# Two blocks of a sequence model on one core: the first modulation goes to TensorE in column groups, and the conv stage's taps and output columns are reordered

## The reference

```
mod   = silu(c) @ w_ada + b_ada            # 6 vectors of 1024; the context has its own, from c_ctx
h     = rmsnorm(x, g_mix) * (1 + scale1) + shift1     (and hc from ctx with the context's vectors)
z     = h @ w_in     # q, k, v, g, dd (decay rank), and three conv and two gate parts
gated linear attention in two directions, started from the context's states; 3-wide conv branch
x     = x + gate1 * (sigmoid(ga)*y_gla + sigmoid(gb)*y_conv) @ w_mix_out
x     = x + gate2 * swiglu(modulate(rmsnorm(x)));  x = rmsnorm(x)
second block: conv/pool mixer (31-wide causal depthwise conv on 512 channels, layernorm, silu,
              window means on the other 512, @ w_out), swiglu, HGRN2 mixer, swiglu, rmsnorm
```

## Time and profile before

| what | us |
|---|---|
| median of 3 runs | 2304.03 (2303.44 to 2307.84) |
| the profiled execution | 2308.86 |
| its span, first to last instruction | 2307.1 |
| PE busy | 2188.2 (95%) |
| DVE / ACT / POOL busy | 1024.4 / 885.7 / 910.2 |

### The profile page before, as it was taken

How to read it: one execution, slowest core, us unless ns; L and a number is a source line. 1 busy time by engine, 2 the same in 40 slices (tenths; PEclk the granted TensorE clock), 3 DMA queues, 4 the chain that set the end, 5 groups by cost and what they waited for, 6 DMA issues and landing times.

```text
span 2307.1 us, 29442 instructions
## 1 busy us (share of the span) xinstructions
PE 2188.2 (95%) x10644; PEld 1763.1 (76%) x10644; DVE 1024.4 (44%) x1421; ACT 885.7 (38%) x1310; POOL 910.2 (39%) x445
## 2 busy tenths in 40 slices
PE   3899999989998999999999999999899989999997
PEld 1788677668886888888757888888688877888886
DVE  7403566565445222212876333300577756333201
ACT  5313435453324222233355233322566645332222
POOL 5222232224444444344543444444322315444442
PEclk8899999999998999999999999999999989999999
DMA  6312121215552322233312322233212213322231
GB/s 240 110 64 64 46 73 41 69 55 189 202 205 87 109 91 100 77 95 92 114 37 74 104 96 94 79 99 111 65 64 73 73 37 104 97 94 97 79 100 67
DMA packets 64703, 217.36 MB, mean 94 GB/s; under 512 B 7008, under 2 KB 8160, under 8 KB 64384
## 3 DMA queue, kind: packets, MB, share of 16 engines
q1 hardware_dynamic: 64640, 216.52, 28.7%
HBM read 214.40 MB, written 2.10 MB: 94 GB/s over the span
## 4 chain that ended last, share of the span: by engine, by line
PE 69%; DVE 5%; ACT 3%; issue 2%; DMA 1%; DVEq 0%; ACTq 0%; SPq 0%
PE ps L473 22%; PE ps L474 21%; PE ps L475 21%; DVE acc L1633 1%; PE ps L767 1%; PE ps L857 1%; DVE h_lo L1596 1%; DMA x_res<-in_x 1%; ACT w_hi L947 0%; ACT h_hi L1146 0%; DVE hs L1878 0%; PE ps L709 0%; PE ps L624 0%; DVE x L1608 0%; PE ps L636 0%
## 5 line engine op out<-in xcount | busy, mean ns | idle before, releaser
L361 POOL TENSOR_TENSOR w_lo<-w_raw,w_hi 128x1024 fp32r<-128x1024 f32 (+2 forms) x376 | 856.7, 2287 | 1341.5 <-ACT w_hi L947 1341.2
L473 PE MATMUL ps<-h_hi,w_lo 128*128 128x512 f32 x1920 | 757.3, 394 | 16.1 <-DVE h_lo L1654 5.0
L475 PE MATMUL ps<-h_hi,w_hi 128*128 128x512 f32 x1920 | 750.8, 391 | 0.0
L474 PE MATMUL ps<-h_lo,w_hi 128*128 128x512 f32 x1920 | 750.6, 391 | 0.0
L947 ACT ACTIVATE w_hi<-w_raw 128x1024 fp32r<-128x1024 f32 (+2 forms) x376 | 370.9, 995 | 507.3 <-PE ps L475 504.4
L473 PEld LDWEIGHTS ps<-h_hi,w_lo 128*128 128x128 f32 x1920 | 363.0, 189 | 100.7 <-DVE h_lo L1654 6.6
L475 PEld LDWEIGHTS ps<-h_hi,w_hi 128*128 128x128 f32 x1920 | 362.3, 189 | 76.5
L474 PEld LDWEIGHTS ps<-h_lo,w_hi 128*128 128x128 f32 x1920 | 363.1, 189 | 74.5 <-issue 0.7
L473 PE MATMUL ps<-gu_hi,w_lo 128*128 128x512 f32 x528 | 205.4, 389 | 0.0
L474 PE MATMUL ps<-gu_lo,w_hi 128*128 128x512 f32 x528 | 205.4, 389 | 0.0
L475 PE MATMUL ps<-gu_hi,w_hi 128*128 128x512 f32 x528 | 205.4, 389 | 0.0
(11 more groups left out here) (330 smaller groups left out, 2469.2 us busy)
## 6 DMA issues: line engine op xcount, KB each, us to landing
w_raw<-in_w_ffn_in SPq DMA_DIRECT2D x132, 512.0 KB, 3.4
ada_w<-in_w_ada SPq DMA_DIRECT2D x48, 512.0 KB, 4.9
w_raw<-in_w_hg SPq DMA_DIRECT2D x40, 512.0 KB, 3.4
w_raw<-in_w_ffn_out SPq DMA_DIRECT2D x48, 384.0 KB, 3.1
w_raw<-in_w_conv_gate SPq DMA_DIRECT2D x32, 512.0 KB, 3.4
w_raw<-in_w_merge SPq DMA_DIRECT2D x32, 512.0 KB, 5.1
w_raw<-in_w_ffn_out SPq DMA_DIRECT2D x48, 320.0 KB, 2.9
w_raw<-in_w_cp SPq DMA_DIRECT2D x20, 512.0 KB, 3.4
```

Source lines behind the costliest of these rows:

```text
L361: pool.tensor_tensor(w_lo[s][:, 0:n], raw[s][:, 0:n], w_hi[s][:, 0:n].bitcast(F32), ALU.subtract).then_inc(lo_done[s], 1)
L473: pe.matmul(out, wl, hi, start=first, stop=False)
L474: pe.matmul(out, wh, lo, start=False, stop=False)
L475: return pe.matmul(out, wh, hi, start=False, stop=last)
```

## The change

**First stage.** The first 2048 columns of `w_ada` are laid out on the host as eight tiles of 128 x (8 x 256): for slice k, the shift and the scale columns. `mod_sums(k)` on PE multiplies them with `cond_pad` (silu of both conditions, padded with zeros to 32 columns): eight f32 matmuls, the chunk j of the inputs writing to the 32 output partitions from 32 j, two chunks accumulated in each. DVE copies the four partial rows out of PSUM (`turn_in`), two small matmuls with a selection matrix `pick` add them and turn them into columns (`mod_turn`), DVE adds the bias and makes `amp1`. DVE (not POOL) now multiplies with `rstd0` and the amplitude in one operation (`value`), ACT adds the shift and rounds (`h1_hi`), DVE takes the low half with the shift in one operation (`low`); only then does it copy the sums for slice k + 2. The squares of x are added in pairs on DVE, so that PE has four matmuls of ones and not eight.

SP loads x first in four pieces, then weight unit and modulation tile in turn, ctx last, and `w_up` only behind `dd_hi`. PE works by pairs (unit, slice): stage k takes slice k for the units so far and all slices so far for unit k (the decay product is unit 4). The context is normalized behind that: its squares are summed inside the last stage, its slices are split by ACT between the reads of q and by DVE; units 4 and 5 run latents, latents, context, context, and then the decay product of the context. The two first units of the next round are converted in `act_start`. The forget gate's small vectors (`lb`, `om_lb`) are made at the end of the qkv stage.

**Conv stage.** The first four tap matrices are made by ACT ahead of its last four weight conversions; the sums of groups 0 and 1 are issued after 24 taps, group 3 ahead of group 2. In the output, slices 0 and 1 go over all units as before, then PE waits for all low halves and finishes unit after unit with slices 2 and 3.

Elsewhere semaphores are only shared or renumbered. The diff, without removed lines (they stand in the code above), cut to its core:

```diff
+    sp.dma_start(cond_col[:, :, :], dram["cond_cols"]).then_inc(S["small_in"], 16)
+    for i in range(4):
+        sp.dma_start(x_all[:, 2 * i:2 * i + 2, 0:T], dram["x"][:, 2 * i:2 * i + 2, :]).then_inc(S[f"x_in{i}"], 16)
     sp.dma_start(vec[:, :], dram["vectors"]).then_inc(S["vec_in"], 16)
+    def ada(k):
+        if k >= 4:
+            sp.wait_ge(S["ada1_used"], k - 3)
+        sp.dma_start(ada1_w[k % 4][:, :, :], dram["w_ada_first"][k]).then_inc(S[f"ada_full{k % 4}"], 16)
+    for s in range(4):
+        sp_unit(sp, s, 0, dram["w_qkv"][0, s])
+        ada(s)
     sp.dma_start(dd_raw[:, :], dram["w_decay"]).then_inc(S["dd_in"], 16)
+    for k in range(4, KC):
+        ada(k)
+    sp.dma_start(x_all[:, :, T:TC], dram["ctx"]).then_inc(S["x_in0"], 16)
     sp.wait_ge(S["const_step"], 1)
+    sp.wait_ge(S["dd_hi"], 1)
     for d in range(2):
         sp.dma_start(w_up[16 * d:16 * d + 16, d, :, :], dram["w_dec_up"][d]).then_inc(S["dd_in"], 16)
...
+    step(pool.memset(cond_pad[:, :, :], 0.0))
...
+    for j in range(3):
+        step(pool.tensor_tensor(pick[:, :], (pick if j else ident)[:, 0:2], ident[:, 32 * j + 32:32 * j + 34], ALU.add))
...
+def pool_first(pool):
+    for s in range(4):
+        pool_lo(pool, s, 0)
     pool.wait_ge(S["dd_hi"], 1)
     pool.tensor_tensor(dd_lo[:, :], dd_raw[:, :], dd_hi[:, :].bitcast(F32), ALU.subtract).then_inc(S["dd_split"], 1)
...
+    def mod_sums(k):
+        pe.wait_ge(S[f"ada_full{k % 4}"], 16 * (k // 4 + 1))
+        if k == 0:
+            pe.wait_ge(S["cond_ready"], 1)
+        if k == 1:
+            pe.wait_ge(S["norm_rstd"], 1)
+        if k >= 2:
+            pe.wait_ge(S["mod_row"], k - 1)
+        for t in range(2):
+            for j in range(4):
+                rows = slice(32 * j, 32 * j + 32)
+                mm = pe.matmul(ps[rows, 5 - k % 2, 0:2 * P], cond_pad[:, j + 4 * t, :], ada1_w[k % 4][:, j + 4 * t, :],
+                               start=(t == 0), stop=(t == 1), skip_group_check=True)
+        mm.then_inc(S["ada1_used"], 1)
+    def mod_turn(k):
+        pe.wait_ge(S["mod_row"], k + 1)
+        if k:
+            pe.wait_ge(S["mod1_ready"], 2 * k - 1)
+        for n in range(2):
+            mm = pe.matmul(ps[:, 7, 4 * k + 2 * n:4 * k + 2 * n + 2], mod_row[k % 2][:, n * P:(n + 1) * P], pick[:, :],
+                           start=True, stop=True, skip_group_check=True)
+        mm.then_inc(S["mod_turned"], 1)
+    begun = set()
+    def pair(s, k):
         pe.wait_ge(S["h_lo"], k + 1)
+        if s < 4:
+            if s not in begun:
+                pe.wait_ge(lo_done[s], 1)
+            mm = products(pe, ps[:, s, :], s, k, h1_hi[:, k, :], h1_lo[:, k, :], s not in begun, k == KC - 1)
+            if k == KC - 1:
+                mm.then_inc(unit_done[s], 1)
+        else:
+            if s not in begun:
+                pe.wait_ge(S["dd_split"], 1)
+            decays(ps[:, 6, :], k, h1_hi, h1_lo, s not in begun)
+        begun.add(s)
...
+    def stage(k):
+        if k > 4:
+            return [(s, k) for s in range(5)]
+        return [(s, k) for s in range(k)] + [(k, i) for i in range(k + 1)]
+    def pairs(some):
+        for s, k in some:
+            pair(s, k)
+    for i in range(4):
+        pe.wait_ge(S["norm_pair"], i + 1)
+        pe.matmul(ps[:, 4, :], ones[:, :], sq0[2 * i][:, :], start=(i == 0), stop=(i == 3)).then_inc(S["sq0_mm"], 1)
+        if i == 2:
+            mod_sums(0)
+    for k in (0, 1):
+        mod_turn(k)
+        mod_sums(k + 1)
+    for k in range(KC - 2):
+        work = stage(k)
+        if k:
+            mod_sums(k + 2)
+        if k == 0:
+            mod_turn(2)
+            pairs(work)
+        else:
+            pairs(work[:1])
+            mod_turn(k + 2)
+            pairs(work[1:])
+    pairs(stage(6))
+    pairs(stage(7)[:1])
+    pe.wait_ge(S["mod_row"], KC - 1)
+    for k in range(KC):
+        pe.wait_ge(S["ctx_sq"], k + 1)
+        pe.matmul(ps[:, 5, 0:CTX], ones[:, :], sqc[k % 6][:, :], start=(k == 0), stop=(k == KC - 1))\
+          .then_inc(S["sq0_mm"], 1)
+    pairs(stage(7)[1:])
...
+    def lat(u):
         s, q, bank = u % 4, u // 4, u % 2
         pe.wait_ge(lo_done[s], q + 1)
         pe.wait_ge(S["qkv_lat_read"], u if u >= 6 else u - 2)
         for k in range(KC):
+            products(pe, ps[:, bank, :], s, k, h1_hi[:, k, :], h1_lo[:, k, :], k == 0, k == KC - 1)
+    def context(u):
+        s, bank = u % 4, u % 2
+        pe.wait_ge(*((S["qkv_ctx_read"], u - 5 if u < 8 else u - 4) if u >= 6 else (S["qkv_lat_read"], u)))
         for k in range(KC):
+            if u == 4:
+                pe.wait_ge(S["split_lo"], k + 1)
        ...
...
+    lat(4)
+    lat(5)
+    context(4)
+    context(5)
+    pe_decay_ctx(pe)
+    for u in range(6, 16):
+        lat(u)
+        context(u)
...
+    def ln_sum(j, sem, n, first=False, last=False):
+        pe.wait_ge(S[sem], n)
+        return pe.matmul(ps[:, 5, :], ones[:, :], cv[:, j, :], start=first, stop=last)
     pe.wait_ge(S["conv_in0"], 2)
     for i in range(CONVW):
+        if i == 24:
+            ln_sum(0, "conv_end", 1, first=True)
+            ln_sum(1, "conv_end", 2)
         pe.wait_ge(S["tap_ready"], i + 1)
         pe.matmul(ps[:, 4, :], tap[i % 4][:, :], a_sb[:, 2, i:i + T], start=(i == 0), stop=(i == CONVW - 1))\
           .then_inc(S["tap_mm"], 1)
+    ln_sum(3, "conv_end", 3)
+    ln_sum(2, "conv_pe", 1, last=True).then_inc(S["ln_sum"], 1)
...
+    for k in range(2):
+        pe.wait_ge(S["cat_lo"], CPC + k + 1)
         for s in range(4):
+            output(s, k)
+    pe.wait_ge(S["cat_lo"], CPC + CPC)
+    for s in range(4):
+        output(s, 2)
+        output(s, 3).then_inc(unit_done[s], 1)
...
 def act_start(act):
     act.wait_ge(S["small_in"], 16)
     act.wait_ge(S["const_ready"], 1)
+    act.activation(cond_pad[:, :, 0:2], cond_col[:, :, :], ACT.Silu).then_inc(S["cond_ready"], 1)
     for k in range(KC):
+        if k % 2 == 0:
+            act.wait_ge(S[f"x_in{k // 2}"], 16)
+        act.activation(sq0[k][:, :], x_all[:, k, 0:T], ACT.Square, scale=ROOT).then_inc(S["norm_sq"], 1)
+    act_hi(act, 0, 0)
+    act.activation(spare[:, 8:9], ones[:, 0:1], ACT.Ln)
+    act.wait_ge(S["sq0_mm"], 4)
+    act_rstd(act, 0, rstd0[:, 0:T], ps[:, 4, :])
+    def ctx_squares(first, last):
+        for k in range(first, last):
+            if k >= 6:
+                act.wait_ge(S["sq0_mm"], 4 + k - 5)
+            act.activation(sqc[k % 6][:, :], x_all[:, k, T:TC], ACT.Square, scale=ROOT).then_inc(S["ctx_sq"], 1)
+    for k in range(KC):
         act.wait_ge(S["h_val"], k + 1)
+        act.activation(h1_hi[:, k, :], nv0[k % 2][:, :], ACT.Identity, bias=mod1[:, k, 0:1]).then_inc(S["h_hi"], 1)
+        if k < 3:
+            act_hi(act, k + 1, 0)
+        if k == 3:
+            act.wait_ge(S["dd_in"], 16)
+            act.activation(dd_hi[:, :], dd_raw[:, :], ACT.Copy).then_inc(S["dd_hi"], 1)
+    act.wait_ge(S["x_in0"], 32)
+    ctx_squares(0, 6)
+    act_hi(act, 0, 1)
+    ctx_squares(6, KC)
+    act.activation(spare[:, 8:9], ones[:, 0:1], ACT.Ln)
+    act.wait_ge(S["sq0_mm"], 4 + KC)
+    act_power(act, rstd0[:, T:TC], ps[:, 5, 0:CTX], S["ctx_rstd"], 0)
+    act_hi(act, 1, 1)
+def act_ctx(act, first, last):
+    for k in range(first, last):
+        act.wait_ge(S["split_val"], k + 1)
+        act.activation(hc_hi[:, k, :], nvc[k % 2][:, :], ACT.Identity, bias=mod1[:, k, 1:2]).then_inc(S["split_hi"], 1)
...
+        if u == 2:
+            act.wait_ge(S["dd_mm"], 1)
+            act.activation(dd_sb[:, 0:T], ps[0:32, 6, :], ACT.Copy).then_inc(S["qkv_lat_read"], 1)
...
+            act_ctx(act, 2 * u, 2 * u + 2)
...
 def act_cp(act):
+    def tap_weights(i):
+        act.activation(tap[i % 4][:, :], ident[:, :], ACT.Copy, scale=v_at("dw_w", 2 * CONVW + i))\
+           .then_inc(S["tap_ready"], 1)
     for r in range(2):
         q = 2 * r + Q_CPI
         for p in range(2):
             act.wait_ge(S["cp_scaled"], 4 * r + 2 * p + 1)
             act.activation(csg[p][:, :], csg[p][:, :], ACT.Sigmoid).then_inc(S[f"conv_sg{p}"], 1)
+            if r == 1 and p == 0:
+                for i in range(4):
+                    tap_weights(i)
             act_hi(act, 2 * p, q + 1)
             act_hi(act, 2 * p + 1, q + 1)
         if r == 0:
             for s in range(4):
                 act_hi(act, s, Q_CPI + 2)
+    for i in range(4, CONVW):
+        act.wait_ge(S["tap_mm"], i - 3)
+        tap_weights(i)
...
+    for i in range(4):
+        dve.wait_ge(S["norm_sq"], 2 * i + 2)
+        dve.tensor_tensor(sq0[2 * i][:, :], sq0[2 * i][:, :], sq0[2 * i + 1][:, :], ALU.add).then_inc(S["norm_pair"], 1)
+    def turn_in(k):
+        dve.wait_ge(S["ada1_used"], k + 1)
+        dve.tensor_copy(mod_row[k % 2][:, :], ps[:, 5 - k % 2, 0:2 * P]).then_inc(S["mod_row"], 1)
+    def modulation(k):
+        both = slice(k, 2 * KC, KC)
+        dve.wait_ge(S["mod_turned"], k + 1)
```

(54 more changed lines are left out.)

228 lines of the change are left out of this document (69 added, 159 removed).

## The result

| | before | after |
|---|---|---|
| median, us | 2305.94 (2303.44 to 2314.06, 4 runs) | 2276.2 (2274.87 to 2278.52, 4 runs) |
| the profiled execution, its span | 2308.86, 2307.1 | 2274.92, 2273.2 |
| mean granted clock | 0.979 | 0.986 |

The ratio is 0.9866 [0.9839, 0.9894]: 29.7 us faster by the medians. Two later comparisons of the same pair gave 0.987 [0.9848, 0.9892] and 0.9865 [0.985, 0.988], 31.9 and 30.6 us. The forecast was 2276.7, a gain of 27.3.

The account below looks back on a forecast made before the run. PE, busy 95% of 2307.1 us, bounds the kernel, so only its waits matter. First stage 20.1 plus conv stage 7.2 gives 27.3 us gained, from a median of 2304.03 to 2276.7; range 2266 to 2293.

Parts of the forecast that it names:

- The round: First stage, PE: eight f32 mod_sums matmuls in four column groups take 1.9 us; ends 3.43 and 0.86.
- rival (A): Modulation rounds: four column groups run at once, 0.86 instead of 1.9 us a round; 2271 or 2268 us; chance 0.20.
- The clock: First stage: PE without gaps from 35 to 70 us at a granted clock of 1.00.
- Rival (C): First stage: PE sinks to the 1.2 GHz level and stays, +28 us, 2304 to 2305; chance 0.05 shared with (E).
- The start: First stage: slice 0 high at 23.9 us, its low half at 24.7; first product at 24 to 26.
- The slices: First stage: the first four slices come 5.2 us apart, as amp must wait for POOL's weight split.
- Stretched in slices 0 to 3: First stage, sign to look for on DVE: amp stretched in slices 0 to 3 and short behind.
- What is late next: Ahead of unit 4: PE waits 2.5 us for q_sb, plus 1.3 us for 1.2 GHz behind it.
- Nothing lost behind it: Behind the first stage: later w_qkv loads cost nothing; moved lb/om_lb chain nothing, or 2 us without cover.
- (B): First stage: column groups don't overlap, or DVE loses POOL turns at values and low halves; 2284 to 2293 us; chance 0.25.
- (D): First stage: low clock and column groups one behind another, 6.9 us a round; slower, 2324 us; chance 0.05.
- (E): Order of queues: added matmuls and taps aren't where the diff puts them; no size; chance 0.05 shared with (C).

Follow-up runs that it names:

- e4: The changed kernel, unchanged, profiled again as the measure for other runs on the same chip; 2276.11 us.
- e7: The changed kernel plus extra 128-column PE matmuls on constants into an unread bank, filling PE's waits in the first stage; 2273.11 us, one run.
- e5: The changed kernel with all eight matmuls of a modulation round in column group 0, three quarters of the inner sum left out; 2291.9 us, one run.
- e3: The changed kernel with ACT reading q of units 0 and 1 around the context's root, ahead of a weight split; 2272.76 us against 2276.11.
- e10: The kernel before with only the conv output's new column order, without the early taps and sums; 2306.03 us, one run, against 2306.63.
- e1: The changed kernel with the conv stage of before, so only the first stage changed; 2281.09 us against 2308.01 for the kernel before, ratio 0.9889.

## Why the prediction was right

**First stage, 20.1 forecast, 21.3 measured.** The path was the one described, but two terms were off and made up for each other. From the low half of slice 0 (24.7 forecast) to the end of the stage (70.4) the prediction has 45.7 us. The profiled execution has 22.92 to 68.64, again 45.7, but by shorter rounds and a lower clock; e4 and e7 have 43.6. That the stage came so close is in part luck.

- *The round.* 1.9 us were forecast, from the 1.8 times of two groups. It takes 1.07, so four groups run 3.4 times as fast as one (e5). This was rival (A)'s mechanism, at a little less than its size; the estimate of 1.1 from the Trainium skill (TensorE: Matmul & The Clock Gate, Part 3: Packing small matmuls) was the better one, and its rule on program order cost nothing. Six rounds at 0.83 less are 5.0 us. With the clock at 1.00 (e7) the stage ended at 66.3, 4.1 ahead of the 70.4 forecast. Two rounds of the profiled execution did take 1.94, near the forecast 1.9, but because of the low clock.
- *The clock.* 1.00 was forecast from 35 us on, and so it was from 40; but it was 0.53 and 0.78 from 20 to 40, which no term held. The profiled execution ended the stage 68.64 - 66.31 = 2.3 us later than e7, 2.1 of it behind slice 0. e4's 1.6 us stand ahead of slice 0, in the sums of squares, where the prediction did reckon with the low clock. Rival (C) had the mechanism but priced it at 28 us: PE had enough to do for the clock to come back by itself. The reading behind it left out one window, where the kernel before had shown that too:

```profile
50.00:60.00 10.00, 4.16 (x16) 3.13 (x14) 9.82 (x9) 4.49 (x8) 10.00 (x5) 0.84 0.17 52
```

- *The start.* `h_lo` of slice 0 was to be ready at 24.7 and was at 22.17 + 0.75 = 22.92; the first two rounds account for most of it (in e4 it was ready only at 24.25). The first product, at 24.63, came within the 24 to 26 us named. A table load of 1.28 us at 7.27 (for silu of the conditions) was overlooked and hid behind the loads.
- *The slices* were to be 5.2 us apart and were 4.8 to 5.6. The POOL turn at `amp` is real (e7), though in the profile of after it hardly shows (0.53, 0.23, 0.23), since there the turned column itself was later than POOL. "Stretched in slices 0 to 3" was thus not seen where the prediction said to look. Its reading that a copy out of PSUM isn't held up rested on a copy at 113.73, when POOL was idle (from 109.41 to 115.36), so it was untested; the copies and `mod` of e7 bear it out.
- *What is late next.* A wait of 2.5 us for `q_sb` was forecast, and 2.36 came; 1.3 us for the low clock behind it, and e7 shows 1.6. Cost of both: about 3 us, as e3 got them back (3.35 by the medians, 3.0 in the trace).
- *Nothing lost behind it.* w_qkv loads issued later, `lb` and `om_lb` at the end of the qkv stage: the shift was 21.3 at 92 us and 21.2 at 210.
- *Two sums* are out by 0.1 us without any effect: stage 2 and the round before it come to 5.3 us, not to less than 5.2, and the end of the two units to 93.5, not 93.6.

**Conv stage, 7.2 forecast, 7.0 measured.** 5.2 for taps and sums against 5.0 (5.05 alone), 2.0 for the columns against 2.0 (2.1 alone), tap 4 late by 0.20 instead of 0.3, and the third DVE column (ended 1164.84) just out of the way of its sum at 1165.17. That DVE's chain, and not PE's wait, carries the second part was the step that could have failed by 1.3 us; e10 shows that it held.

**The total, 27.3 forecast.** Changed code gave 28.3. The medians say 29.7, 30.6 and 31.9. The 1.4 to 3.6 us beyond have no place in changed code; the profiles show stretches of unchanged code, with the clock granted differently from execution to execution, that differ by as much. e1 shows that such a gain can come with the first stage alone (26.9 by the medians, 20 to 22 in the trace). Whether the change makes them likelier, by shifting everything behind it, or whether it was the draw, is open. The 2276.7 is closer than its parts: the base of 2304.03 was the median of three runs, and the later ones gave 2305.9 to 2308.0, so a base 2 to 4 us low met a gain 2 to 5 us low: that the total was hit to 0.5 us is luck.

**The rivals.** (A) came true in its size of a round and not in its time, for the clock took half. (B) is out: groups overlap, and values and low halves kept their 0.75 us; only `amp` lost part of a turn, 0.57 to 1.05 us a slice in e7. (C) and (D) are out by the clock of 1.00 from 40 us on. (E) is out by PE's timeline, where rounds, turns and taps stand in the order of the diff.
